# Seven-product form for the projections in the middle of both hybrid layers, with the 31-tap convolution accumulated in PSUM in pieces of ten taps

## The reference

```python
h = rms_norm(x, norm1_g)
q, k, v, iq, ik, iw, a_in, c_in, g_in = jnp.split(h @ w_in, IN_SPLITS, axis=-1)
... q, k are normalised and rotated; iq, ik, iw choose 64 keys for each token ...
y_attn = dsa_attention(q, k, v, iq, ik, iw) @ w_attn_out
a_val, a_gate = jnp.split(a_in, 2, axis=-1)
a = causal_dwconv(a_val * sigmoid(a_gate), conf_conv_w) + conf_conv_b     # 31 taps, 1024 channels
y_conf = silu(layer_norm(a)) @ w_conf_out
c_b, c_c, c_x = jnp.split(c_in, 3, axis=-1)
y_sc = (c_b * causal_dwconv(c_c * c_x, sc_conv_w)) @ w_sc_out             # 3 taps
gates = sigmoid(g_in.reshape(B, S, 3, 1024))
x = x + (gates[0] * y_conf + gates[1] * y_attn + gates[2] * y_sc) @ w_o
... then a gated FFN with a 3-tap convolution ...
```

## Time and profile before

| | |
|---|---|
| median of 3 runs | 2019.89 us (2019.89 to 2020.93) |
| profiled execution, own time | 2019.41 us |
| its span | 2017.6 us |
| PE busy | 2003.7 us, 99% |
| DVE busy | 1055.7 us, 52% |
| POOL busy | 782.2 us, 39% |
| ACT busy | 403.7 us, 20% |

### The profile page before, as it was taken

How to read it: one execution, slowest core, us unless ns; L and a number is a source line. 1 busy time by engine, 2 the same in 40 slices (tenths; PEclk the granted TensorE clock), 3 DMA queues, 4 the chain that set the end, 5 groups by cost and what they waited for, 6 DMA issues and landing times. The chain is left out here.

```text
span 2017.6 us, 34732 instructions
## 1 busy us (share of the span) xinstructions
PE 2003.7 (99%) x13230; PEld 1836.6 (91%) x13230; DVE 1055.7 (52%) x2702; ACT 403.7 (20%) x986; POOL 782.2 (39%) x537
## 2 busy tenths in 40 slices
PE   9999999999999999999999999999999999999999
PEld 7788889888889999999888888999999999899998
DVE  4244446974343567514992454557823366555541
ACT  2231521112111222111122122032202014220000
POOL 1000042000002487765000000668875774248873
PEclk9999999999999999999999999999999999999999
DMA  5314444344334455444444433444454443345444
GB/s 209 128 45 144 146 149 148 132 152 146 132 140 142 151 170 169 172 146 161 134 147 150 146 128 123 170 165 168 162 173 148 145 147 105 126 146 183 171 159 136
DMA packets 42960, 298.32 MB, mean 148 GB/s; under 512 B 4928, under 2 KB 6080, under 8 KB 8832
## 3 DMA queue, kind: packets, MB, share of 16 engines
q1 hardware_dynamic: 42560, 295.42, 42.7%
q10 hardware_dynamic: 256, 0.92, 0.3%
HBM read 294.35 MB, written 1.05 MB: 146 GB/s over the span
## 5 line engine op out<-in xcount | busy, mean ns | idle before, releaser
L708 PE MATMUL bank<-xn,ring 128*128 128x256 f32 (+2 forms) x3776 | 686.4, 340 | 0.5 <-DMA ring<-wstream 0.5
L708 PEld LDWEIGHTS bank<-xn,ring 128*128 128x128 f32 x3776 | 610.2, 190 | 69.0 <-issue 4.6
L708 PE MATMUL bank<-arena,ring 128*128 128x128 f32 (+2 forms) x3702 | 641.4, 328 | 4.3 <-DVE arena L1711 2.4
L708 PEld LDWEIGHTS bank<-arena,ring 128*128 128x128 f32 x3702 | 564.2, 191 | 62.3 <-issue 3.5
L708 PE MATMUL bank<-arena 128*128 128x128 f32 (+3 forms) x2264 | 298.1, 287 | 0.0
L708 PEld LDWEIGHTS bank<-arena 128*128 128x128 f32 (+1 forms) x2264 | 274.9, 192 | 9.3 <-issue 1.5
L708 PE MATMUL bank<-arena,h_res 128*128 128x128 f32 x1960 | 234.5, 276 | 1.9 <-POOL h_res L1676 1.2
L708 PEld LDWEIGHTS bank<-arena,h_res 128*128 128x128 f32 x1960 | 225.7, 192 | 4.5 <-POOL h_res L1676 2.4
L1711 DVE SCALAR_TENSOR_TENSOR arena<-arena,par (+2 forms) x536 | 214.6, 475 | 0.3
L1667 POOL TENSOR_TENSOR h_res<-ring 128x512 f32<-128x512 f32 x12 | 15.5, 1294 | 495.2 <-issue 363.0
L1672 POOL TENSOR_TENSOR arena<-ring 128x1024 f32<-128x1024 f32 (+1 forms) x70 | 167.0, 2385 | 89.7 <-DMA ring<-wstream 89.7
(11 more groups left out here) (224 smaller groups left out, 1624.6 us busy)
## 6 DMA issues: line engine op xcount, KB each, us to landing
ring<-wstream SPq DMA_DIRECT2D x264, 1024.0 KB, 4.8
ring<-wstream SPq DMA_DIRECT2D x16, 768.0 KB, 4.2
cst<-consts SPq DMA_DIRECT2D x1, 2488.0 KB, 14.7
h_res<-tokens SPq DMA_DIRECT2D x2, 544.0 KB, 5.3
out<-arena SPq DMA_DIRECT2D x4, 256.0 KB, 5.4
arena<-arena ACTq DMA_DIRECT2D x4, 160.0 KB, 3.8
ring<-wstream SPq DMA_DIRECT2D x2, 288.0 KB, 2.8
par<-params SPq DMA_DIRECT2D x1, 541.5 KB, 9.2
```

Source lines behind the costliest of these rows:

```text
L708: return pe.matmul(o, lhs, rhs, start=start, stop=stop, skip_group_check=True)
```

## The change

28 plain blocks of each layer (`q` 4, `kv` 2, `iq` 2, `g` 12, `conf` 4, `sc` 4) become fast blocks; `a0`, `ik`, `cx0`, `cx1`, `cb`, `attn0`, `o0` and `up0` stay plain. The convolution is no longer a loop over SBUF: its 248 steps (8 tiles by 31 taps) accumulate in bank 4, ten steps behind each `unite` and the last 38 behind `spread_norm`. So the side banks that PE takes in that stretch are 5, 6 and 7 only (`"beside"`). The centring, the variance and the indexer's products move behind `cx0`; the short convolution moves from the heads to the stretch before them; `cb` is multiplied straight out of PSUM; and two new sets of activation sums appear, `yc` (before the heads) and `ys` (in head 1). ACT's gate Tanh now runs over the united pairs.

```diff
-        pl(n + "q", "w_in_2", l, 2, 2, 8, seq(qo))
-        pl(n + "kv", "w_in_2", l, 1, 2, 8, seq(ko))
-        pl(n + "iq", "w_in_2", l, 1, 2, 8, seq(iqo))
+        fast(n + "q", "w_in_2", l, 4, 1, lambda it, q: qo + 256 * it)
+        fast(n + "k", "w_in_2", l, 1, 1, lambda it, q: ko)
+        fast(n + "v", "w_in_2", l, 1, 1, lambda it, q: vo)
+        fast(n + "iq", "w_in_2", l, 2, 1, lambda it, q: iqo + 256 * it)
         pl(n + "ik", "w_in_2", l, 1, 1, 8, lambda it, q: span(iko, 72))
-        pl(n + "g0", "w_in_2", l, 3, 2, 8, seq(go))
-        pl(n + "g1a", "w_in_2", l, 1, 2, 8, seq(go + 1536))
-        pl(n + "g1b", "w_in_2", l, 2, 2, 8, seq(go + 2048))
+        fast(n + "g", "w_in_2", l, 12, 1, lambda it, q: go + 256 * it)
...
-        pl(n + "conf", "w_conf_out_2", l, 2, 2, 8, seq(0))
-        pl(n + "sc", "w_sc_out_2", l, 2, 2, 8, seq(0))
+        fast(n + "conf", "w_conf_out_2", l, 4, 1, lambda it, q: 256 * it)
+        fast(n + "sc", "w_sc_out_2", l, 4, 1, lambda it, q: 256 * it)
...
+        if kind == "beside":
+            self.turn["side"] += self.turn["side"] % 4 == 0
+            kind = "side"
...
-                blocks(L + "g0", 8, x256, S)
-                blocks(L + "g1a", 8, x256, S)
-                row_spread(L + "qk", 5, 1)
+                fast_stage(F, "g", 12, 1, of_tokens(xn), (F, "x"), None)
+                row_spread(L + "qk", 5, 1, "beside")
+                blocks(L + "cx0", 8, x256, S)
                 centre_sums(L + "ln", 1, lambda j: sel[:, 0, :], [(L + "ln", "total")])
-                blocks(L + "g1b", 8, x256, S)
...
+                def convolved(lo, hi):
+                    for n in range(lo, hi):
+                        j, k = 2 * (n // (2 * CK)) + n % 2, n % (2 * CK) // 2
+                        acc, weight = both_p[:, n % 2, :], G(g("conf_conv_w_2"), CK * j + k)
+                        if k == 0:
...
+                        else:
+                            dve.wait_ge(*e.at((L + "tap", j, k - 1)))
+                            stt(ac[:, j, :] if k == CK - 1 else acc, cp[:, j, k:k + S], weight, acc, ALU.mult,
+                                ALU.add).then_inc(*e.step((L + "ac", j) if k == CK - 1 else (L + "tap", j, k)))
...
+                for it in range(12):
+                    unite((F, "g", it, 0), sg[:, 2 * it:2 * it + 2, :], 0)
+                    convolved(90 + 10 * it, 100 + 10 * it)
                 spread_norm(L + "qk", 5, lambda p: g("q_norm_g_2" if p < 4 else "k_norm_g_2"), qk0, qk0, L + "qkn")
...
+                convolved(210, 8 * CK)
...
                 def branches_part(h):
 
+                    if h == 1:
+                        for j in range(ND):
+                            dve.wait_ge(*e.at((L + "ys", j)))
+                        token_sums((F, "ys"), ys)
                     if h == 0:
...
+                    unite((F, part, n, 0), both_p, 0, *([(F, "branch", h - 1)] if h > 1 else []))
```

More of the change, by code:

```diff
@@ L158, in down_quarters @@
     return quarters(w, 256 * it, [2 * k for k in DOWN_PAIRS[q]], 1)
-FAST = [f"L{l}.{part}" for l in range(2) for part in ("a", "attn", "o", "up", "down")]
+FAST = [f"L{l}.{part}" for l in range(2) for part in ("a", "q", "k", "v", "iq", "g", "conf", "sc", "attn", "o", "up", "down")]
 FAST += [f"C.{part}" for part in ("mqk", "mv", "rqk", "rv", "rg", "gate", "ret", "o", "up", "down")]
@@ L606, in causal_heads @@
             pts = probt3 if L == "C." else probt2
+            side = "side" if pair else "beside"
             def logits(h):
@@ L628, in output @@
                 pe.wait_ge(*e.at((L + "pts", h)))
-                for event in ([(("C", "mv", 1, 0), part) for part in ("c11", "c12", "c22")] if pair else [(L + "v2",)]):
+                for event in ([(("C", "mv", 1, 0) if pair else (L[:2], "v", 0, 0), part) for part in ("c11", "c12", "c22")]):
                     pe.wait_ge(*e.at(event))
-                b = e.take("side", (L + "o", h))
+                b = e.take(side, (L + "o", h))
                 pe.wait_ge(*e.emptied((L + "o", h)))
@@ L874, in unscaled, with row_sums @@
                            between=None if q else totals, late=2 if T == S and q == 0 else 0)
-            def row_sums(key, n, weights, per):
-                b = e.take("side", (key, "sum"))
+            def row_sums(key, n, weights, per, kind="side"):
+                b = e.take(kind, (key, "sum"))
                 pe.wait_ge(*e.emptied((key, "sum")))
@@ L884, in row_sums, with row_spread @@
                 ins.then_inc(*e.side_done((key, "sum")))
-            def row_spread(key, pairs, per):
+            def row_spread(key, pairs, per, kind="side"):
                 i0 = CONST["ident"][0]
@@ L890, in row_spread @@
                 for p in range(pairs):
-                    b = e.take("side", (key, "spread", p))
+                    b = e.take(kind, (key, "spread", p))
                     pe.wait_ge(*e.emptied((key, "spread", p)))
@@ L1076, in _ @@
                 i0 = CONST["ident"][0]
-                b = e.take("side", (L + "iw",))
+                b = e.take("beside", (L + "iw",))
                 pe.wait_ge(*e.emptied((L + "iw",)))
@@ L1109, in _ @@
                         ins.then_inc(*e.side_done((L + "idx", t, j)))
-                blocks(L + "cb", 8, x256, S)
+                blocks(L + "cx1", 8, x256, S)
+                b = e.take("beside", (L + "ln", "var"))
+                pe.wait_ge(*e.emptied((L + "ln", "var")))
+                for n, (event, j) in enumerate((((L + "ln", "acc"), 0), ((L + "ln", "sq", 6), 6), ((L + "ln", "sq", 7), 7))):
+                    pe.wait_ge(*e.at(event))
+                    ins = mm(b, slice(0, P), slice(0, S), C("ones"), sq[:, j, 0:S], n == 0, n == 2)
+                ins.then_inc(*e.side_done((L + "ln", "var")))
+                for q in range(4):
+                    halves(L + "cb", q, 8, [P, P], x256, S)
                 for event in [(L + "yc", j) for j in range(ND)]:
@@ L1114, in branch_block @@
                 def branch_block(h):
[L1116 to L1122, removed]
+                    part, buf, sums = ("conf", yc, "yc") if h < 4 else ("sc", ys, "ys")
+                    fast_block((F, part, h % 4, 0), (F, part, h % 4, 0), of_tokens(buf), (F, sums),
+                               ready=[(L + "ys", j) for j in range(ND)] if h == 4 else None)
                 causal_heads(e, pe, mm, L, 8, lambda h: qk0[:, h, :], lambda h: qk0[:, 8 + h // 4, :],
@@ L1423, in _, with squares_of @@
                                    scale=0.5).then_inc(*e.step((F, "ag", it)))
[L1424 to L1439, removed]
+                def squares_of(block, first):
+                    for part in ("c11", "c12", "c22"):
+                        act.wait_ge(*e.at((block, part)))
+                    act.activation(sq[:, first:first + 2, 0:S], qk0[:, first:first + 2, :],
+                                   ACT.Square).then_inc(*e.step((L + "qk", "sq", first + 1)))
+                for it in range(4):
+                    first_product((F, "q", it, 0))
+                    if it >= 1:
+                        squares_of((F, "q", it - 1, 0), 2 * it - 2)
+                first_product((F, "k", 0, 0))
+                squares_of((F, "q", 3, 0), 6)
+                first_product((F, "v", 0, 0))
+                squares_of((F, "k", 0, 0), 8)
+                for it in range(2):
+                    first_product((F, "iq", it, 0))
+                for part in ("c11", "c12", "c22"):
+                    act.wait_ge(*e.at(((F, "iq", 1, 0), part)))
                 act.wait_ge(*e.at(("iq", "zero")))
@@ L1455, in _, with products_in @@
                     act.dma_start(qk[a:a + 16, :, :], qk0[b:b + 16, :, :]).then_inc(qk_halves, 16)
[L1456 to L1462, removed]
+                def products_in(c):
                     with e.turns(f"{L}cx{c}", 2) as i:
@@ L2294, in branches_part @@
[L2294 to L2297 removed]
+                        return
+                    n, part = (h - 1) % 4, "conf" if h <= 4 else "sc"
+                    tiles = slice(2 * n, 2 * n + 2)
+                    gate = sg[:, 2 * n + (0 if h <= 4 else 16):2 * n + (2 if h <= 4 else 18), :]
+                    unite((F, part, n, 0), both_p, 0, *([(F, "branch", h - 1)] if h > 1 else []))
```

221 lines of the change are left out of this document (113 added, 108 removed).

## The result

| | median | runs | ratio to before |
|---|---|---|---|
| before | 2019.89 us | 5, 2019.79 to 2020.93 | |
| changed | 2029.62 us | 5, 2029.16 to 2031.64 | 1.0049, 95% interval [1.0035, 1.0063] |

A forecast was written before the change was run, and what follows sets the result against it. PE's work was taken to bound the kernel. From 2019.41 us, 37.5 gained less 2 x (3.9 + 3.2 + 3.7) gave 2003.5, plus 0.48 for the median 2004.0 us; range 1994 to 2015.

The forecast's parts named there:

- the sum: Whole kernel: 37.5 us gained on PE less three stalls in each of two layers, 21.6, leaves 15.9 us.
- rival (D): PE's clock falls to 1.2 GHz behind stalls, 2.9 us each; six cost 17.4, giving 2021 us; chance 0.20 in all.
- The gain: PE, 56 blocks: each goes from 6.92 to 6.25 us, 37.5 us in all if PE never waits.
- rival (C): Stretch of 20 blocks: DVE becomes the bound if taps stretch to 0.47 us; 11.6 us lost, 2016 us; chance 0.13.
- Loss 1: `row_spread`: PE idles 3.9 us before the fourth pair, bounds 2.7 and 4.5, while DVE finishes a `unite` and ten taps.
- Loss 2: Index products: PE loses 3.2 us, bounds 2 and 4, because mean, centring and squares now precede the first Relu.
- Loss 3: Head 1, before PE's transposes: DVE's four sums, contended by POOL's mixing, stall PE 3.7 us.
- with one of the four free: Head 1: one of DVE's four sums taken as uncontended by POOL, so the stall is 3.7 us, not 4.4.
- the 2.41 us wait: PE's longest wait in the profile before; behind it 103 records ran at the full clock, 0.218 us each.
- five or six falls: Part of rival (D): clock falls behind five or six of six stalls; chance 0.06, against 0.14 for one to four.
- one of the signs that I had named: Sign that the forecast is wrong: records behind a stall take 0.22 us for 128 columns in place of 0.11.
- The third `cb` block: PE after `cx1`: finds its banks free with 0.3 us to spare, costed at nothing; at most 2 us per layer.

The follow-up runs named there:

- the kernel with all three away: Changed kernel with spreads read before the last ten taps, head 1's sums dealt over heads 0 to 3, index products ahead of the norm: 1984.39 us, again 1985.13.
- with fillers: Changed kernel with 8, 9 and 14 multiplications that nothing reads put into its six long waits: 2016.63 us, ratio 0.9979.
- the single removals: Changed kernel with one wait per layer taken away at a time: head 1's 2013.03 us, the fourth spread's 2020.24 us, the index products' 2014.4 us.
- a filler: In the run meant here, the changed kernel with 4, 5 and 9 multiplications that nothing reads put into its six waits: 2019.93 us, ratio 0.9998.

## Why the prediction was wrong

The step that failed is the sum, 37.5 - 2 x (3.9 + 3.2 + 3.7): it has no term for TensorE's clock, which stood only in rival (D). The runs showed 18.0 us there, more than the 15.9 of the whole forecast gain, and by that alone the kernel comes out slower. The waits that I subtracted were 6.9 us too short besides. One by one:

**The gain: right.** With the waits away the span is 2017.6 - 1981.7 = 35.9 us under that of before, for a forecast of 37.5 without any wait. Fast gate blocks stand 6.25 us apart. DVE's 640 taps average 483 ns, the 484 of the earlier trace rows, and no `unite` fell behind in the gate stretch; rival (C) had no part in it.

**The places of the waits: right. Their sizes: three terms.** *Loss 1*, forecast 3.9: 3.77 in both layers. *Loss 2*, forecast 3.2, bounds 2 to 4: 4.19 and 4.08, just above the upper one. I had put the centring at 2.77 us; it took 4.36. The squares that ACT now makes beside it set POOL to adding 1.4 us into it. Before, that adding began as the centring ended (the first line is of the kernel before, the others of the changed one):

```profile
452.62 3.95 POOL L1640 TENSOR_TENSOR sq<-sq 128x256 f32<-128x256 f32 x5 [22.79 <-ACT sq L1237]
...
498.31 4.36 DVE L2062 TENSOR_TENSOR arena<-arena,tmp 128x256 f32<-128x256 f32 x8
...
499.68 4.37 POOL L1638 TENSOR_TENSOR sq<-sq 128x256 f32<-128x256 f32 x5 [13.08 <-ACT sq L1235]
```

In the changed kernel four of the eight operations are about done when POOL starts, 1.37 us in, and the rest take 2.99; before, all eight took 416 to 424 ns each. So the pace halves where the adding begins. That is a coincidence in time, in this trace and in each of those with the centring moved (4.37 to 4.38 us); no run takes the adding away. *Loss 3*, forecast 3.7, bounds 1.0 to 4.4: 6.38, beyond its upper bound. What failed in this term is "with one of the four free". None was free, and the division's last two operations (L2004), behind them, were stretched too, from 0.55 us before to 1.25:

```profile
575.99 1.49 DVE L2125 TENSOR_TENSOR xn<-arena 128x512 f32<-128x512 f32 x1 [0.22 <-issue]
577.51 2.72 DVE L2127 TENSOR_TENSOR xn<-xn,arena 128x512 f32<-128x512 f32 x1
580.27 1.64 DVE L2129 TENSOR_TENSOR xn<-arena,xn 128x512 f32<-128x512 f32 x1
581.84 1.75 DVE L2130 TENSOR_TENSOR xn<-arena 128x512 f32<-128x512 f32 x1
...
586.23 1.25 DVE L2004 TENSOR_SCALAR arena<-arena,small 128x128 f32<-128x128 f32 x2
```

That is 7.6 us for four sums that take 0.69 each with POOL idle, where the 3.7 of the forecast left 5.5 for them. In the kernel that deals them out the same operations took 0.68 us at 573.95 and 591.24, where POOL waits for a load, and 1.76 at 582.88, where it mixes. The sum of the three losses was 21.6 for both layers; 28.5 were there. By that alone the forecast would have been 2011, still faster.

**The clock: the case that I gave 0.06.** Rival (D) had the mechanism, and its price was right in the sum: 2.9 us each, six times, 17.4; measured 18.0 (from the busy time of the same records with and without the waits) and 17.3 (with fillers). That 2.9, taken from the start of the program, fits so well is partly luck: place by place the price was about 2 to 5 (below). What failed is the chance. I let one row speak, the 2.41 us wait behind which the clock stayed up in one execution, and gave five or six falls 0.06 against 0.14 for one to four, as if each were a toss of its own. They have one cause, and all six waits were longer than the longest that I had seen pass. One of the signs that I had named came with it: records of 128 columns behind a stall took about twice their time, 11 in 2 us where 20 are done later. By the sentence of the Trainium skill's page "TensorE: Matmul & The Clock Gate" (Why this matters for your kernels) on idle gaps between bursts of matmuls this rival should have been the forecast. The traces agree with it at the waits of 3.8 to 6.4 us; the falls behind waits of 1.75 and 2.4 us go beyond it. With the waits as forecast and (D)'s price, 2021; the 7 us by which the waits were too short bring it to 2028, and 2029.6 was measured; the gain was 35.9 and not 37.5.

The account, by spans: -35.9 for the blocks, +28.1 for idle time, +18.0 for the clock is +10.2 = 2027.8 - 2017.6.

**The third `cb` block** found its banks, as forecast, but with more to spare than the 0.3 us that I had added up. The product that frees them ends at 551.74 us, and PE, which starts the first block at 539.22, is through with the second two blocks of 6.92 later, at about 553.1: an estimate of 1.3 us. With the centring moved in front of it and the product left late, PE waits 4.04 us there.

## What to carry to other kernels

Where one engine is busy all the time, a wait of 4 to 6 us cost its own length and some 2 to 5 us of clock behind it, and the second part is not in the waits' table; look for it in the granted clock of the windows behind the bracket, and in records that take twice as long. So a change that makes the work denser should be costed with each new wait at its length plus a fall of the clock, and all falls as one case, not as independent ones. Three reorderings that cost nothing (a read before ten taps rather than behind them, four operations dealt out over four heads, products ahead of an independent norm, with the `cb` product moved up beside them) turned 0.5% slower into 1.8% faster; where a wait can't be taken away, work that nothing reads gives back the second part.

## What the runs showed of the hardware

The price of a fall differs by place. From PE's busy time in the single removals it is 2.1 us behind the spread. The other two of those executions had a fall at the old wait besides, which cost 1.2 us of busy time (1969.4 and 1968.2 in the two profiles of the kernel with all three away); with that added, an estimate, it is 2.5 behind head 1's wait and 4.6 behind the index products. Twice 2.1 + 2.5 + 4.6 is 18.4, and 18.0 was measured for all six. Behind the wait for the `cb` banks it was 1.7. The windows show 0.50 for about 5 us behind the spread, and from 503 to 511 us behind the index products. These, which use 64 of 128 rows, kept the clock low longest. A wait of only 1.75 us, 1.64 in the second layer, between a filler and sixteen of them came with a fall in both layers, where waits of 2.05 and 2.44 us ahead of matmuls over all 128 rows did not. What of their form does it, no run here parts. And the same wait of 2.4 us brings a fall in some executions of one program and none in others. The two profiled spans differ by 2.3 us, and this seems to be a large part of the spread between this kernel's runs, since filling the wait narrowed them to 0.25 us.
